# Two of eight feature tiles of a causal convolution computed by GpSimd instead of VectorE

## The reference

```
u = glu_a * jax.nn.sigmoid(glu_b)
ext = jnp.concatenate([buf0.astype(u.dtype), u], axis=1)
c = lax.conv_general_dilated(ext, conv_w[:, None, :].astype(ext.dtype), window_strides=(1,),
                             padding='VALID', dimension_numbers=('NWC', 'WIO', 'NWC'),
                             feature_group_count=D_CONV) + conv_b
cn = (cf - mu) * lax.rsqrt(var + EPS) * conv_ln_g.astype(jnp.float32) + conv_ln_b.astype(jnp.float32)
y_a = jax.nn.silu(cn).astype(h.dtype) @ w_conv_out
...
S_new = jnp.exp(L * lg)[None, :, None, None] * S + jnp.einsum('bjhd,bjhe->bhde', k_dec, v)
```

## Time and profile before

| What | us |
|---|---|
| median of 3 runs (lowest, highest) | 778.12 (777.89, 778.29) |
| profiled execution: its time | 778.71 |
| profiled execution: its span on the core | 776.8 |
| busy in the span: TensorE, VectorE, ScalarE, GpSimd | 755.2, 667.5, 514.4, 97.1 |

### The profile page before, as it was taken

The page is one execution under the profiler, slowest core; times in us unless marked ns, Lnnn a source line. Parts: engine busy times, 40 slices in busy tenths (PEclk is TensorE's granted clock), DMA queues, the critical chain, the costliest instruction groups (busy, mean ns, idle before and its releaser), DMA issues.

```text
span 776.8 us, 12114 instructions
## 1 busy us (share of the span) xinstructions
PE 755.2 (97%) x4731; PEld 656.4 (84%) x4731; DVE 667.5 (86%) x908; ACT 514.4 (66%) x649; POOL 97.1 (12%) x120
## 2 busy tenths in 40 slices
PE   8999999999999999999999999999999999999994
PEld 4999999877777799999889966888888888888873
DVE  5699999888889887999868676998899989999897
ACT  7433445876877874345595553788888888888863
POOL 0100001233333200000011001011111111110000
PEclk9999999999999999999999999999999999999998
DMA  8935547599899944554448563999999999999972
GB/s 343 363 124 191 182 163 244 188 348 341 300 324 308 342 167 162 190 189 163 163 165 328 201 271 114 353 366 373 374 379 353 360 377 384 354 367 355 365 270 78
DMA packets 39174, 213.28 MB, mean 275 GB/s; under 512 B 7381, under 2 KB 7637, under 8 KB 19244
## 3 DMA queue, kind: packets, MB, share of 16 engines
q1 hardware_dynamic: 23268, 165.39, 57.8%
q0 software_dynamic: 15408, 45.71, 16.6%
q10 hardware_dynamic: 432, 1.31, 0.4%
HBM read 193.45 MB, written 31.65 MB: 290 GB/s over the span
## 4 chain that ended last, share of the span: by engine, by line
PE 83%; DVE 12%; ACT 3%; issue 2%; DMA 1%; DVEq 0%; ACTq 0%
PE bank L1612 34%; PE bank L1888 34%; DVE conv L1155 3%; DVE w_lo L1108 3%; PE bank L1878 2%; PE bank L1670 2%; PE bank L1758 2%; PE bank L1723 1%; PE bank L1776 1%; PE bank L1638 1%; PE bank L1918 1%; PE bank L1797 1%; PE bank L1790 1%; DMA con<-constants 1%; PE bank L1629 1%
## 5 line engine op out<-in xcount | busy, mean ns | idle before, releaser
L1612 PE MATMUL bank<-h_hi,w_hi 128*128 128x264 f32 (+1 forms) x640 | 188.9, 295 | 3.5 <-DVE w_lo L1108 3.3
L1612 PE MATMUL bank<-h_lo,w_hi 128*128 128x264 f32 (+1 forms) x640 | 184.9, 289 | 0.0
L1612 PE MATMUL bank<-h_hi,w_lo 128*128 128x264 f32 (+1 forms) x640 | 184.8, 289 | 0.0
L1113 DVE TENSOR_TENSOR ring_lo<-raw,ring_hi 128x2048 fp32r<-128x2048 f32 x72 | 163.6, 2288 | 22.5 <-ACT ring_hi L770 22.5
L1108 DVE TENSOR_TENSOR w_lo<-raw,w_hi 128x1024 fp32r<-128x1024 f32 x112 | 136.7, 1221 | 27.5 <-ACT w_hi L763 26.8
L763 ACT ACTIVATE w_hi<-raw 128x1024 fp32r<-128x1024 f32 x112 | 117.9, 1052 | 55.9 <-PE bank L1612 53.7
L770 ACT ACTIVATE ring_hi<-raw 128x2048 fp32r<-128x2048 f32 x72 | 138.2, 1920 | 19.2 <-PE bank L1888 19.2
L1612 PEld LDWEIGHTS bank<-h_hi,w_hi 128*128 128x128 f32 x640 | 121.3, 190 | 7.2 <-DVE w_lo L1108 5.0
L1612 PEld LDWEIGHTS bank<-h_lo,w_hi 128*128 128x128 f32 x640 | 121.2, 189 | 0.8 <-issue 0.2
L1612 PEld LDWEIGHTS bank<-h_hi,w_lo 128*128 128x128 f32 x640 | 121.0, 189 | 0.0
L1155 DVE SCALAR_TENSOR_TENSOR conv<-u,vec,conv 128x256 f32<-128x256 f32 x240 | 101.8, 478 | 0.6
(11 more groups left out here) (302 smaller groups left out, 1481.3 us busy)
## 6 DMA issues: line engine op xcount, KB each, us to landing
raw<-weights SPq DMA_DIRECT2D x152, 1024.0 KB, 7.0
S_ring<-in_state_ret POOLq DMA_DIRECT2D x20, 512.0 KB, 7.5
out_ret_sample<-S_ring POOLq DMA_DIRECT2D x20, 512.0 KB, 6.8
xT<-in_state_ret POOLq DMA_DIRECT2D x8, 512.0 KB, 6.1
out_ret_sample<-xT POOLq DMA_DIRECT2D x8, 512.0 KB, 7.4
S_five<-in_state_ret POOLq DMA_DIRECT2D x4, 512.0 KB, 5.0
out_ret_sample<-S_five POOLq DMA_DIRECT2D x4, 512.0 KB, 9.7
out_ret_prompt<-S_out POOLq DMA_DIRECT2D x8, 256.0 KB, 5.9
```

Of the source, the lines that this page charges most:

```text
L1113: dve.tensor_tensor(ring_view(ring_lo, k), raw[raw_slot(NCM + k)][:, :].rearrange("p (k n) -> p k n", k=4), ring_view(ring_hi, k).bitcast( ...
L1612: ins = pe.matmul(out, a[:, k, cols], b[:, k0 + k, :], start=first and k == 0 and j == 0, stop=last and k == ks - 1 and j == 2)
```

## The change

Tiles 2 and 3 of the convolution (`POOL_CONV`) leave VectorE's list, which falls from 248 steps to 186. GpSimd computes them: per tap and tile a product (`tensor_scalar`) into a scratch buffer and an addition (`tensor_tensor`) of that to the tile; the first tap is a product plus the bias straight into the tile. The scratch lies in slot 3 of `S_ring`. So state 3 cannot be loaded before the convolution is done, and `load(3)` moves behind it; the loads of states 4 to 6 stand behind `load(3)` in GpSimd's program. VectorE waits for GpSimd's part before it sums for the layer norm.

```diff
+POOL_CONV = (2, 3)
...
-            for n in range(4):
+            for n in range(3):
                 load(n)
+            for f in POOL_CONV:
+                evacuated(pool, ("m", UNIT[("glu_a", f)]))
+            for t in range(CW):
+                for i, f in enumerate(POOL_CONV):
+                    w_t = cw[:, f, t:t + 1]
+                    out, src = conv[:, f, NMETA:TP], u[:, f, NMETA + t:t + TP]
+                    part = S_ring[:, 3, i, 256 * (t % 2):256 * (t % 2) + 256]
+                    if t == 0:
+                        pool.tensor_scalar(out, src, w_t, par[:, PAR["conv_b"] + f:PAR["conv_b"] + f + 1], ALU.mult, ALU.add).then_inc(conv_pool, 1)
+                    else:
+                        pool.tensor_scalar(part, src, w_t, None, ALU.mult).then_inc(tap_pool, 1)
+                if t:
+                    for i, f in enumerate(POOL_CONV):
+                        out, part = conv[:, f, NMETA:TP], S_ring[:, 3, i, 256 * (t % 2):256 * (t % 2) + 256]
+                        pool.wait_ge(tap_pool, 2 * (t - 1) + i + 1)
+                        pool.wait_ge(conv_pool, 2 * (t - 1) + i + 1)
+                        pool.tensor_tensor(out, out, part, ALU.add).then_inc(conv_pool, 1)
+            pool.wait_ge(conv_pool, 2 * CW)
+            load(3)
             pool.wait_ge(rot_ready, 8)
             for n in range(4, SLOTS):
                 load(n)
...
-                    convs += [(2 * p, t), (2 * p + 1, t)]
+                    convs += [(f, t) for f in (2 * p, 2 * p + 1) if f not in POOL_CONV]
...
-                    dve.wait_ge(conv_step, KT * CW)
+                    dve.wait_ge(conv_step, len(convs))
+                    dve.wait_ge(conv_pool, len(POOL_CONV) * CW)
```

More of the change, by code:

```diff
@@ L487, in build @@
         cc_ready, csq_ready, cz_ready, chi_ready, clo_ready, csig_ready = (sem(n) for n in ("cc_ready", "csq_ready", "cz_ready", "chi_ready", "clo_ready", "csig_ready"))
+        conv_pool, tap_pool = sem("conv_pool"), sem("tap_pool")
         conv_step, osb_ready, rot_ready, x2_ready = sem("conv_step"), sem("osb_ready"), sem("rot_ready"), sem("x2_ready")
```

## The result

| What | before | after |
|---|---|---|
| median (lowest, highest), us | 778.0 (775.77, 778.29) | 819.07 (816.42, 821.7) |
| span of the profiled execution, us | 776.8 | 819.6 |
| ratio of the times, 95% interval | | 1.0538 [1.052, 1.0555] |

Slower by 5.4%, 41 us; the forecast was 818.5. The number came out, and the way to it only in part: some 28 us are what GpSimd takes from VectorE, and some 18 are a wait for the late state 3, which the forecast had given to a rival. The four runs of the changed kernel lie near 816.5 and near 821.5, and the profile is one of the latter (821.39). I go through it in the order in which the causes show.

A forecast was written before the change was run, and what follows sets the result against it. VectorE was taken to set the end ahead of the layer norm and to be within 1.3 us of it from 43 to 135; 40 - 1.3 + 5 - 3.3 = +40.4 us gave 818.5, range 774 to 845.

The forecast's parts named there:

- a rival: Late load: GpSimd's train ends too late and ScalarE waits for state 3 at 144 us; 785 to 830, chance 0.15.
- VectorE sets the end from 43 to 135 us, and every microsecond added is paid: Units of glu, q, k, first v: VectorE busy 90.66 of 92 us, within 1.3 us of setting the end.
- The gain of 3.3 us at the sum: Ahead of the layer norm: 0.25 + 1.29 us of TensorE idle time and 1.7 us of low clock come back.
- One pass for a product, two for an addition, 52 us in all: GpSimd's train from 42.2 us: 62 products at 0.32 us and 60 additions at 0.54, priced from a memset's pass.
- the 88 that I had called the upper bound: GpSimd's 122 instructions at 0.72 us each, the time for issuing a load.
- Taking turns costs VectorE all of GpSimd's work less 12 us, 40 us: From 43 to about 145 us, GpSimd's work and VectorE's two-input work alternate; 52 - 12 = 40 us lost; chance 0.58.
- load(3) is then in time: With turns taken, GpSimd ends near 145 us, and the need for state 3 has moved back by 39 us.
- 5 us for the clock: TensorE, idle 2 us in each 5 beside the train, gets a lower clock: between 0 and 22 us, taken as 5.
- What would show it wrong: w_lo keeping 1.22 us beside GpSimd's additions, or GpSimd's instructions alone, while VectorE rests, taking over 0.72 us.
- w_lo at 1.5 us or more: Sign of turns taken: from 43 to about 145 us w_lo takes this instead of 1.22, or has long gaps ahead.
- 43.7 us were forecast as contention: Up to state 3: VectorE's 40 us of loss, less 1.3 us idle, plus 5 us for the clock.

The follow-up runs named there:

- prod48: The kernel before plus 48 unused GpSimd products (128x256, one tensor read) where the train stands in the changed kernel; 783.75 us, 1.0076.
- add48: The kernel before plus 48 unused GpSimd additions (two tensors read) where the train stands in the changed kernel; 793.71 us, 1.0204.
- split23: The changed kernel with GpSimd's taps 0 to 22 ahead of load(3) and the last eight behind the last state store; 806.36 us, 1.0384.

## Why the prediction came out, and where it did not

- **VectorE sets the end from 43 to 135 us, and every microsecond added is paid.** Right where the load is in time, as in prod48, add48 and split23: VectorE stayed full while the train ran, and TensorE stood idle behind it. In the changed kernel VectorE is full too and 28.3 us late, but GpSimd's train took longer still and sets the end.
- **The gain of 3.3 us at the sum.** Right in size: the six early steps alone give 3.7, and in the changed kernel the windows are full and 4.1 us come back at the layer norm. Of the sum, 1.7 us were the clock's, and these fall due only in some of the executions. That 46.3 us at state 3 became 42.8 at the end, 3.5 less, is no second measurement of the gain; it is made up of +2.0, -4.1 and some -1.5.
- **One pass for a product, two for an addition, 52 us in all.** Wrong, and this is the step that failed. Alone, products take 0.91 and additions 0.70 us: 98 us, over the 88 that I had called the upper bound. The bound was a row of another kind of instruction (issuing a load), which bounds nothing; and the memset from which I took the pass writes only.
- **Taking turns costs VectorE all of GpSimd's work less 12 us, 40 us.** The mechanism was right, as seen instruction by instruction; the size was not. It is 28.3 us of GpSimd's 98: GpSimd waits longer than VectorE, 45 us over the train (1.50 us for a product of 0.91), and of what it holds only a part falls on VectorE.
- **load(3) is then in time.** Wrong: 18.0 us late at 190.32. I had tied a late load to a VectorE that keeps its pace, and the turns to a load in time. Both happened: the train is too long, and VectorE too slow.
- **5 us for the clock.** Not to be separated. From 43 to 150 it fell only to 0.94, in one window; from 150 to 175 it was 0.86 and from 175 to 200, most of it in the wait, 0.73, and what that cost is inside the 18 us or right behind them.
- **What would show it wrong.** I wrote that the forecast is wrong if GpSimd's instructions alone take over 0.72 us. They do. w_lo at 1.5 us or more was a sign of turns taken, and it is 1.33 with the loss in conv. So where 43.7 us were forecast as contention, 28.3 are contention and 18.0 lateness: that 818.5 is so close to 819.07 is luck, since two errors cancel, the contention (with its clock) 15 us too dear and the load 18 us too cheap.

The Trainium skill, SBUF — State Buffer, section "Who interferes with whom", has statements that the runs now test. That a two-input VectorE instruction and a GpSimd instruction that reads SBUF contend, and that whoever issues first holds what they share for the whole instruction: agreed as to the contention, conv 0.96 instead of 0.48 us beside an addition; who was first can't be read off these rows, where the product that starts 0.23 us ahead of w_lo waits for it. That a GpSimd instruction which only writes does not contend with a two-input one: agreed, 0.9988 with 160 memsets. That a reduction never contends and a product or sum with a constant can, in those of its modes that take the shared ports: the reduction agrees (0.40 us), and the other was kept out not for one instruction but for the rest of the train, 70.61 us. The rule of turns made into "all of GpSimd's time is VectorE's loss" was my step, and the runs give 28.3 us of the train's 98.

## What to carry to other kernels

Before work goes to GpSimd beside a full VectorE, measure one instruction of its kind alone and one beside VectorE; the second is what its train takes, and the time of a memset tells neither. Look at what is queued behind the train on the same engine: a load that was free at the start of the program becomes ScalarE's longest wait, 18 us, when 143 us of arithmetic stand ahead of it. And when the gain sought is a gap of under 2 us at one place, moving six instructions on the busy engine to units with room gives it without a second engine.

## What the runs showed of the hardware

- A VectorE addition with one tensor input and a per-partition constant (128x8, 0.23 us) stood 70.61 and 103.32 us beside back-to-back GpSimd memsets, until the last, though the same instruction at the start of the train took 0.35; with a second tensor input it took 0.17 us beside the same train. A reduction with one input (0.40 us) was not touched.
- The same addition took 0.23 to 0.37 us beside GpSimd products and 0.65 beside GpSimd additions.
- A GpSimd product of 128x256 by a per-partition factor took 0.91 us alone and 1.50 beside VectorE; an addition of two such tensors 0.70 and 0.86.
- 48 such products made VectorE 6.6 us later and 48 additions 16.6, though the products took nearly twice as long.
- 160 memsets of 128x512, 75 us of GpSimd's time, cost nothing beside two-input instructions (0.9988 of the time of the kernel before).
- After the same 1.8 us of idle TensorE at the layer norm, the granted clock fell to 0.57, 0.50 and 0.50 in three profiles and stayed at 1.00 in three others; the first cost 1.5 us more.
